# Issuing the down weights of each expert on ScalarE's queue, once the expert before is done with the buffers

## The reference: what is computed

```
combine = jnp.sum(jax.nn.one_hot(ids, N_EXPERTS, dtype=jnp.float32) * gates[..., None], axis=1)
hg = jnp.einsum('nd,edf->nef', xt, w_gate)      # 16 experts, 2048 -> 512
hu = jnp.einsum('nd,edf->nef', xt, w_up)        # 16 experts, 2048 -> 512
a = jax.nn.silu(hg) * hu * combine[:, :, None].astype(x.dtype)
out = jnp.einsum('nef,efd->nd', a, w_down)      # 16 experts, 512 -> 2048
```

## Time and profile before

| | |
|---|---|
| median of 3 runs | 1012.3 us (1011.66 to 1013.6) |
| the profiled execution | 1012.74 us, of which the span (first to last instruction) 1010.9 us |
| mean granted TensorE clock | 0.923 |
| PE busy | 843.4 us, 83% of the span |
| DVE, ACT, POOL busy | 258.0, 215.8, 78.4 us |
| mean DMA traffic | 281 GB/s over the span; over 400 GB/s in the slices of the experts |

### The profile page before, as it was taken

The page is one execution under the profiler, slowest core; times in us unless marked ns, Lnnn a source line. Parts: engine busy times, 40 slices in busy tenths (PEclk is TensorE's granted clock), DMA queues, the critical chain, the costliest instruction groups (busy, mean ns, idle before and its releaser), DMA issues.

```text
span 1010.9 us, 11856 instructions
## 1 busy us (share of the span) xinstructions
PE 843.4 (83%) x4598; PEld 551.4 (55%) x4598; DVE 258.0 (26%) x370; ACT 215.8 (21%) x242; POOL 78.4 (8%) x77
## 2 busy tenths in 40 slices
PE   5999999999999999877988777887778788787820
PEld 4989989999999999743333222222222222222210
DVE  5363423335744444450000000000000000000017
ACT  5233412322224232213111101110111011110011
POOL 0100000000000000040111001101110011100005
PEclk8999978999999999777999999989999999998975
DMA  9644322544457442576999999999999999999953
GB/s 285 226 128 132 124 91 86 164 139 151 136 178 237 126 150 99 225 295 223 404 414 412 419 409 404 403 424 407 411 413 421 414 411 413 410 422 407 360 165 113
DMA packets 89965, 284.42 MB, mean 281 GB/s; under 512 B 7146, under 2 KB 59808, under 8 KB 63562
## 3 DMA queue, kind: packets, MB, share of 16 engines
q1 hardware_dynamic: 83676, 265.61, 67.8%
q0 software_dynamic: 4672, 10.51, 4.1%
q10 hardware_dynamic: 1590, 7.92, 2.3%
HBM read 273.64 MB, written 16.78 MB: 287 GB/s over the span
## 4 chain that ended last, share of the span: by engine, by line
PE 54%; DMA 39%; DVE 3%; ACT 1%; issue 1%; SPq 1%; POOLq 0%; ACTq 0%; DVEq 0%
DMA gu_w<-in_expert_w_up 36%; PE ps L426 12%; PE ps L427 12%; PE ps L428 12%; PE ps L1145 10%; PE ps L1165 2%; PE ps L1096 1%; PE ps L1087 1%; DMA x_rows<-tok 1%; DMA tok<-sum_rows 1%; PE ps L512 1%; PE ps L511 1%; DVE tok L1414 1%; SPq L953 1%; DMA sum_rows<-yout,result_row 1%
## 5 line engine op out<-in xcount | busy, mean ns | idle before, releaser
L1145 PE MATMUL ps<-gu_w,xgT 128*64 128x512 f32 x1024 | 252.7, 641 | 67.8 <-DMA gu_w<-in_expert_w_up 66.9
L1145 PEld LDWEIGHTS ps<-gu_w,xgT 128*64 128x64 f32 x1024 | 73.7, 146 | 232.7 <-issue 132.9
L426 PE MATMUL ps<-xT_hi,w_hi 128*128 128x320 f32 x544 | 170.3, 313 | 1.0 <-DVE xT_lo L742 1.0
L427 PE MATMUL ps<-xT_lo,w_hi 128*128 128x320 f32 x544 | 169.5, 312 | 0.0
L428 PE MATMUL ps<-xT_hi,w_lo 128*128 128x320 f32 x544 | 169.5, 312 | 0.0
L571 DVE TENSOR_TENSOR w_lo<-raw,w_hi 128x2048 fp32r<-128x2048 f32 x50 | 114.0, 2288 | 146.1 <-ACT w_hi L565 146.1
L1165 PE MATMUL ps<-down_w,aT 128*64 128x512 f32 x512 | 123.5, 627 | 10.5 <-ACT aT L1243 10.5
L565 ACT ACTIVATE w_hi<-raw 128x2048 fp32r<-128x2048 f32 x50 | 95.3, 1912 | 146.1 <-PE ps L428 142.2
L426 PEld LDWEIGHTS ps<-xT_hi,w_hi 128*128 128x128 f32 x544 | 103.6, 190 | 1.4 <-DVE xT_lo L742 1.1
L427 PEld LDWEIGHTS ps<-xT_lo,w_hi 128*128 128x128 f32 x544 | 103.5, 190 | 0.0
L428 PEld LDWEIGHTS ps<-xT_hi,w_lo 128*128 128x128 f32 x544 | 103.4, 190 | 0.0
(11 more groups left out here) (199 smaller groups left out, 520.1 us busy)
## 6 DMA issues: line engine op xcount, KB each, us to landing
gu_w<-in_expert_w_gate SPq DMA_DIRECT2D x64, 1024.0 KB, 20.1
gu_w<-in_expert_w_up SPq DMA_DIRECT2D x64, 1024.0 KB, 27.5
down_w<-in_expert_w_down SPq DMA_DIRECT2D x64, 1024.0 KB, 26.7
raw<-in_w_in SPq DMA_DIRECT2D x34, 1024.0 KB, 5.2
raw<-in_w_out SPq DMA_DIRECT2D x16, 1024.0 KB, 5.2
tok<-in_x_prompt SPq DMA_DIRECT2D x2, 1024.0 KB, 6.0
x_rows<-tok ACTq DMA_DIRECT2D x2, 1024.0 KB, 5.0
sum_rows<-tok ACTq DMA_DIRECT2D x2, 1024.0 KB, 4.3
```

Of the source, the lines that this page charges most:

```text
L426: pe.matmul(out, wh[:, t, col], hi[:, kt, :], start=(n == 0 and t == 0), stop=False)
L427: pe.matmul(out, wh[:, t, col], lo[:, kt, :], start=False, stop=False)
L1145: last = pe.matmul(ps[C * side:C * (side + 1), GU, :], x, w[:, :, c, FH * side:FH * (side + 1)], start=(j == 0 and c == 0), stop=(j == PAI ...
```

## The change

SyncE's per-expert program issues gate and up only. The four down transfers of expert n + 1 are issued by ScalarE, in its step for expert n, behind its wait for all eight uses of expert n (`ring_used` at `USES * n + USES`) and ahead of the copy of `yout`. So the wait for each down buffer by itself becomes one wait for the last of them. Only the first expert's down weights are still issued by SyncE. (The further rounds over the experts, for more than 64 tokens in one expert, are changed alike.)

```
+    def load_down(eng, e):
+        for f in range(FT):
+            eng.dma_start(down_w[f][:, :].rearrange("p (j d) -> p j d", j=1),
+                          down_v[:, bass.ds(e, 1), f, :].rearrange("p e d -> p e d"))\
+               .then_inc(down_full[f], 16)
+
     def sp_expert(sp, n, e, first):
...
-        for f in range(FT):
-            if not first:
-                wait_alone(sp, ring_used, PAIRS + f + 1 - USES + n * USES, sp_turns)
-            sp.dma_start(down_w[f][:, :].rearrange("p (j d) -> p j d", j=1),
-                         down_v[:, one, f, :].rearrange("p e d -> p e d")).then_inc(down_full[f], 16)
+        if first:
+            load_down(sp, e)
...
             act.wait_ge(ring_used, USES * n + USES)
+            if not last_step:
+                load_down(act, e + 1)
             act.wait_ge(yout_free, n + 1)
             act.copy(yout[:, :].rearrange("p (b c) -> p b c", b=2), ps[:, Y:Y + 2, :]).then_inc(y_read, 1)
...
         def one_round(r):
+            if not isinstance(r, int):
+                load_down(act, 0)
             tokens(r * NE)
```

## The result

The changed kernel takes 1018.3 us (median of 8 runs, 1015.06 to 1023.41) against 1011.98 us before (8 runs, 1010.54 to 1014.87): a ratio of 1.006, with a 95% interval of 1.0036 to 1.0084, so 6 us slower (4 to 9). The forecast was slower, 8.5 us.

What follows compares the result with a forecast made beforehand. Transfers were taken to bound the expert stage, with no loop change; a later last gate/up pair would add 8.5 us: 1012.74 + 8.5 = 1021.2, hence 1021 against the median. Range 1017 to 1024; with one line and most slower cases, 1011 to 1027.

Steps and rivals of the forecast that it cites:

- Bytes bound the experts, so nothing is won or lost within the loop: Expert loop: DMA engines have no gap, so the period stays 32.6 us an expert; worth nothing in either direction.
- rival that two queues move less: Over the experts' 480 us, two loading queues move 1 to 2% less: 1026 to 1031 us; chance 0.13.
- The lateness is covered: When down is issued late, some 3.2 MiB of gate/up are still queued, over 8 us of cover: no gap.
- Equal turns: The two loading queues share the engines equally, so gate and up land last, not down; chance 0.50.
- rival of one line for both queues: Both queues served in order of issue: last pair lands at 955.6, time as before, 1012.5 us (1011 to 1014); chance 0.20.
- The cost is the order at the very end: Expert 15: the last gate/up pair lands at 963.4, not 955.6, with 12.9 us or 1.7 more of PE work behind.
- all weights are in at 965.4 again: End of expert 15's transfers: total bytes and rate as before, so the last weights land at the same time, 965.4.
- Its size, 7.8 to 9.5 us: End of expert 15: PE ends at 976.3 to 978.0 instead of 968.5; 8.5 us taken.
- signs of being wrong: In the changed profile: last pair near 955.6, a period off 32.6 by over 0.3, or PE waiting for down.
- PE asks for down no earlier than 23 us after T: Middle experts: T ends the previous expert's last product; down is in about 20 us after, before PE asks.
- The norm's loads compete only with what isn't urgent: End of expert 15: gain and bias compete only with the last 0.8 MiB of down, wanted 6 us later.
- Four issues on ScalarE cost nothing: Ahead of `yout`, per expert: four issues take 1.3 to 8.4 us, covered; taken as 0.

Runs made afterwards that it cites:

- tail_on_sp: Changed kernel, but the down weights of expert 15 alone issued by SyncE as before: 1013.29 us, ratio 1.0018 to the kernel before.
- late_on_sp: Kernel before, SyncE still issuing down, but only once all eight buffers of the expert are used: 1012.71 us, ratio 1.0007.
- tail_on_act: Kernel before, but expert 15's down weights alone issued by ScalarE, all four once expert 14 is done: 1021.64 us, ratio 1.0097.
- norm_later: Changed kernel, but SyncE issues the second norm's gain and bias only after all down weights have landed: 1020.19 us, ratio 1.005 to before.
- the two runs that tested it: Changed kernel, ScalarE issuing down only from expert 2, or 3, on; tested whether gate/up left, O, becomes 6.5 MiB - O next: 1019.59, 1019.64 us.

## Why the prediction was right, and where it wasn't

- *Bytes bound the experts, so nothing is won or lost within the loop.* Right in the sum: 32.7 us an expert before and after, and tail_on_sp, with 56 of 60 down transfers on the new queue, is 0.2% from before (1.0001 to 1.0034). The rival that two queues move less has its 1% in the GB/s, but no time in the loop. (The 36% of the span that I put down to one transfer are the sum over many up transfers.)
- *The lateness is covered.* Right, by late_on_sp (1.0007).
- *Equal turns, so that gate and up land after down, not ahead of it.* Right: 2.20 against 2.06 MB. The rival of one line for both queues is gone. The place that spoke for it only showed how long a transfer takes to begin. Before, SyncE's refill was issued at 470.40 and q1 moved its first bytes after 473; in the changed kernel it was issued at 468.58, and q1 began after 470, while q10 still had data to move. So both queues were busy in the same window, 471 to 473:

```profile
q1 hardware_dynamic: 53, 0.43, 58.8%
q10 hardware_dynamic: 43, 0.30, 40.1%
```

- *The cost is the order at the very end.* Right, by the pair tail_on_sp (+0.2%) and tail_on_act (+1.0%). That all weights are in at 965.4 again was 3 us off: the last down transfer lands at 968.3, beside the norm's loads. Before, those came behind it and landed last, at 970.3 (941.9 + 28.4). Counted from the first product, the very last of these transfers lands at 506.6 before and 506.0 now, so the bytes as a whole are not later.
- *Its size, 7.8 to 9.5 us.* Measured 6 to 7.5 in three sets of runs. The mis-sized term is where expert 15's last pair starts. I put 963.4, which is 499.7 us after the first product (463.7); the three profiles of the changed kernel have 956.7, 955.3 and 959.3, which is 494.3, 492.9 and 497.2. The work behind it, with the waits for down in it, was 13.6, 14.9 and 15.4 us, where I had 12.9 to 14.6. Only the third of these profiles was taken near the median (1019.5 us; the others 1015.1 and 1015.2), so where the last pair starts in a median run rests on one profile. I had taken the steady state for a fixed point, with every expert at 32.6 us. It is not: the periods run from 27.0 to 38.5, and the last pair lands anywhere around the mean. For tail_on_act, which has one queue up to expert 14, a sum of the same kind held: last pair forecast near 965, found at 962.0 with a first product 2.8 us earlier than before; time 1020 to 1024, found 1021.64.
- *The signs of being wrong.* Two of the three came, in the very first profile. The last pair started at 956.7, within about 1 us of the 955.6 that I had named as the sign of one line, and `yout` of expert 15 at 970.3 and not near 977. Taken alone, this sign would have pointed at the wrong rival; the bytes of the two queues and tail_on_act decide against it. And PE did wait for down, 2.6 us in four places. The step that failed there is that PE asks for down no earlier than 23 us after T. That holds only where it waits long for the last pair. In expert 5 it didn't wait, and asked for the first down buffer 16.9 us after T (619.95 to 636.88) and waited for a later one until 647.53, 27.6 us after T. No run prices these waits by themselves. The third sign, a period off by over 0.3, stayed away.
- *The norm's loads compete only with what isn't urgent.* Off by a little. They are issued at 935, 6 us earlier than before, and in the changed kernel PE waited 0.57 us for the last down transfer. norm_later shows no gain. It doesn't exclude one of 2 us.
- *Four issues on ScalarE cost nothing.* Right: each takes 0.34 us, and PE waits for ScalarE's `aT` 10.6 us in all, before 10.5. 1.8 us pass ahead of `yout`, and they are covered:

```profile
943.43 1.82 ACTq L945 DMA_DIRECT2D down_w<-in_expert_w_down  x4
945.29 1.01 ACT L1253 COPY yout<-ps 128x1024 f32<-128x1024 f32 x1 [4.96 <-issue]
```

- *Missed:* the gather of the next tokens has to share as well. Against two full queues it lands 15.9 us after its issue, not 8.9, and PE waited for it in three places, 6.6 us in all; 4.8 of these are the first expert's gather, which was waited for before as well. The other 1.8 lie in experts in which PE doesn't wait for gate and up, so nothing shows that they cost anything.

What stays open is whether the 6.5 - O argument is the cause of the swing, since the two runs that tested it failed to move the last expert's phase, and what makes the swing slip. What a swing costs without the four last transfers on ScalarE is bounded by tail_on_sp: 0.2% (0.01 to 0.34). No version tried beats the kernel before.

## What to carry to other kernels

In a stage that is bound by transfers, ask what compute still hangs on the last byte. In one queue the weights moved in the order in which they were asked for, and PE never waited for down. With two queues they shared the engines, and the urgent transfer went beside the one that could wait. Here only the last four transfers had to be in the right order: a peeled last step that keeps them on the first queue gives back nearly all of a second queue's cost.

## What the runs showed of the hardware that I had not expected

- With two queues the experts of the changed kernel's first profile alternated between a wait of 5 to 9 us and one of 0 to 4, with the same mean period of 32.7 us. In one queue the waits for gate and up add up to 2.3 to 6.0 us in each of experts 2 to 15.
- Transfers on a third queue got slower when two others were full: the gather's time to landing went from 8.9 to 15.9 us (median), while in late_on_sp, with one queue, it was 9.1. From 593 to 595 in the changed kernel, with all three queues busy, q10, q1 and q0 had 34.9, 33.6 and 32.7% of the engines, a third each:

```profile
L1027 POOL DMA_INDIRECT xg<-x_rows,gather_row x16: 1002/1033/1167, 455.1 to 913.3; - x16
...
DMA to landing us min/median/max: 4.5/15.9/17.0
```

- SyncE's issues no longer stall. With down on ScalarE's queue, issuing an up transfer took SyncE 0.38 us in the middle and 0.69 at most, where before it took 1.31 and 4.36. No saving in time is to be seen from it.

```profile
L959 SPq DMA_DIRECT2D gu_w<-in_expert_w_up x64: 382/383/694, 377.3 to 933.4; - x64
```
